# Conditioning blocks among the first projections, ScalarE evicting the RWKV preparation, and C merged inside the inverse, in a two-layer mixer kernel on one core

## The chip, the cores and the metric

The kernel runs on one NeuronCore of a Trainium2 chip. The metric is the device time of one execution in microseconds (us). TensorE (PE) multiplies matrices, VectorE (DVE) and ScalarE (ACT) do the elementwise work and empty PSUM, GpSimd (POOL) does some masks and starts small DMAs, and SyncE (SP) starts the DMAs of the weights.

## The reference

All arrays are float32, for one sequence of T = 256 tokens of width 1024. The first block projects x into four branches and their gates, merges the branches, normalizes, and adds a mixture of 32 experts with 4 per token. A second block (modulated norm, dilated attention, pooling) follows. What matters here:

```python
z = x @ w_in                                # zA | zB | zC | zD | zG
yA = rwkv7_mix(zA)                          # 8 heads of 64, token shift first
#   a = sigmoid(a0 + xa @ a2)
#   decay = exp(-exp(-softplus(-(w0 + tanh(xw) @ w2)) - 0.5))
#   kk = k * k_k;  kk = kk / max(sqrt(sum(kk * kk)), 1e-12)
#   k = k * (1 + (a - 1) * k_a)
#   state = state * w + (state @ -kk) (kk * a)^T + v k^T ;  y = state @ r
yB, yC, yD = hgrn2_mix(zB), mlstm_mix(zC), rglru_mix(zD)
merged = sum(sigmoid(zG_n) * (y_n @ w_branch_n) for n in ABCD)
x1 = layernorm(ALPHA * x + merged @ w_out)
x2 = layernorm(ALPHA * x1 + moe(x1) + ple(x1, p))
# second block, conditioned on one vector c of 1024:
shift, scale, gate = split(c @ w_ada + b_ada, 3)        # w_ada is 1024 x 3072
h = rmsnorm(x2) * norm_g * (1 + scale) + shift
out = rmsnorm(x2 + gate * (merged2(h) @ w_out2))
```

The three vectors of the conditioning (shift, scale, gate) depend on c alone and are first read in the second block (gate8 and gateB turn the gate into rows earlier).

## The kernel before

One arena of SBUF holds everything by hand-placed offsets. Each engine has one instruction stream, written out in program order, and semaphores tie them. Three ring slots hold the weight units, of 2 MB mostly. SyncE loads them in the order of the list `UNITS` (L111), and unit n waits until unit n - 3 has been used (L503 to L510). TensorE writes into two sets of four PSUM banks, each used round robin in the order of a list: `PROJ` (L121), emptied by ScalarE through `out` (L1347), and `SMALL` (L131), emptied by VectorE through `full`. A bank of either list can be written when the entry four places earlier has been copied out.

TensorE's program is: x turned; the projections of D, C and B by `ones_channels` (L627) and `ones_tokens` (L637), with the small matmuls of the branches between them; the gates of D and the merge of D (`merge`, L648); eight levels of branch B (L764), each beside one half projection of A; the B output (L778), the gate projection G C 0; the RWKV preparation; the inverse; the chunk states and outputs of A with the quarters of the gate G A; the merge of A (ending about 563 us); the output projection `mixed` (L1039), x1 and the router (L1049, L1058), the ple projections (`embed`, L1102), and the expert loop (L1158 to L1208), then the second block.

The RWKV preparation (L782 to L875 of TensorE's program) is this. Low rank products w, a and g (L793) go to `small` banks and VectorE adds the bias (L1829 to L1831). ScalarE takes the sigmoids (L1450, L1451). The squares of the key are summed over each head (L799); ScalarE takes a square root of it (L1453), and VectorE clamps and takes a reciprocal (L1857, L1858). VectorE scans the log decays (L1862, L1863), ScalarE takes three exponentials (L1455 to L1457), and VectorE multiplies them in (L1868 to L1871), signalling `A_tilde` once per product. TensorE turns three of the products to tokens (`to_tokens`, L806), which VectorE copies out (L1876), and forms NT (`pair`, L853), which VectorE masks (L1882). GpSimd multiplies NT with a level mask (L573, once per level, `NTm_ready`), TensorE turns it (X0, `turned_bank`, L875). The inverse has four levels (L883 in the loop over `l`), each of 16 X products, 16 D products and 16 transposes DT; after the first and after the second group stands one quarter of a gate projection (`gate_quarter`, L885), eight quarters of G B in all.

The conditioning has six blocks, one for each 512 columns of w_ada. `ada_rows(i)` (L820) is eight matmuls of 32 equal columns of c against 512 columns of the weight unit; its result is copied to SBUF, and `ada(i)` (L828) turns it to partitions by four matmuls with a one-column operand; VectorE adds the bias (L1818). Blocks 0 to 3 stand between the steps of the RWKV preparation, where VectorE copies the rows (L1814). Blocks 4 and 5 stand between the router's logits and the ple projections, followed by the transpose gate8 (L1082). The merge of C (`merge("C")`) stands whole, as 32 matmuls, between X0 and the inverse. c and its companions are loaded by GpSimd after the merge of D (L561 to L564).

## Time and profile before

| what | us |
| --- | --- |
| median of 3 runs | 1945.26 (1944.66 to 1947.16) |
| the profiled execution, its own time | 1947.88 |
| its span, first to last instruction | 1945.7 |
| granted TensorE clock, mean of the span | 0.975 |
| start of the RWKV preparation's part (last level of B done) | 284.42 |
| end of the inverse's fourth level | 448.47 |
| merge of A done | 563 |
| first expert matmul | 659.02 |
| last expert step done, second block starts | about 1600 |

The page gives for each engine the busy time. The timeline lists instructions in time order, with the idle time before each and the engine that ended it. The stretch table gives busy time and granted clock between two moments: clock 1.00 is 2.4 GHz and 0.50 is 1.2 GHz. A timeline row's count is in records; a matmul of 128 columns by 256 has two records.

### The profile page before, as it was taken

To read this page: it belongs to the slowest core of one execution; us is meant where nothing else is said; L and a number is where in the kernel's file an instruction comes from. 1 tells how busy PE (TensorE), PEld (TensorE's weight loads), DVE (VectorE), ACT (ScalarE), POOL (GpSimd) and SP (SyncE) were. 2 spreads that over 40 slices of the span, in tenths; PEclk is the share of its full clock that TensorE was granted. 3 is DMA by queue.
4 is the path that set the end of the run, shared out by engine and by line. 5 is a ranking of instruction groups with operands and counts; after the bars stand their busy time and mean duration, and the time that the engine had idled before them with its cause. 6 is when DMAs were issued, how large, how long until landed. Compare 5 with 4: busy or idle time off the path is not lost. (4 is left out here: it accounts for less than half of the span.)

```text
span 1945.7 us, 21418 instructions
## 1 busy us (share of the span) xinstructions
PE 1835.1 (94%) x8829; PEld 1074.9 (55%) x8829; DVE 553.8 (28%) x1037; ACT 237.2 (12%) x379; POOL 43.9 (2%) x39
## 2 busy tenths in 40 slices
PE   8999998899999999999999999999999979999998
PEld 7688886699865344333333333333333327768984
DVE  3543486555234211111111111111111130014412
ACT  0322122000100001100101101101101111011100
POOL 1000000130000000000000000000000000000000
PEclk9999998899898999999999999999999989999999
DMA  7443342512138899999999999999999975532331
GB/s 258 147 156 124 105 140 87 189 72 90 47 122 299 351 422 428 428 428 428 429 428 428 428 428 428 429 428 429 427 429 427 429 287 195 165 130 87 103 135 60
DMA packets 94139, 537.69 MB, mean 276 GB/s; under 512 B 5763, under 2 KB 15277, under 8 KB 69385
## 3 DMA queue, kind: packets, MB, share of 16 engines
q1 hardware_dynamic: 88960, 527.53, 67.4%
q10 hardware_dynamic: 3464, 4.85, 0.9%
q0 software_dynamic: 1664, 4.58, 0.8%
q8 instruction: 38, 0.62, 0.1%
q14 instruction: 13, 0.10, 0.0%
HBM read 531.18 MB, written 5.77 MB: 276 GB/s over the span
## 5 line engine op out<-in xcount | busy, mean ns | idle before, releaser
L1176 PE MATMUL small<-arena 128*64 128x512 f32 x2048 | 459.7, 597 | 44.2 <-DMA arena<-in_expert_w_gu 44.2
L1176 PEld LDWEIGHTS small<-arena 128*64 128x64 f32 x2048 | 160.0, 137 | 338.3 <-issue 248.7
L1208 PE MATMUL small<-arena 128*64 128x512 f32 x1024 | 226.8, 594 | 4.6
L2119 DVE TENSOR_SCALAR arena<-small 128x512 f32<-128x512 f32 x32 | 22.1, 692 | 721.7 <-PE small L1183 721.7
L627 PE MATMUL proj<-arena 128*128 128x256 f32 x960 | 211.5, 381 | 0.0
L627 PEld LDWEIGHTS proj<-arena 128*128 128x128 f32 x960 | 182.6, 191 | 25.7 <-issue 1.0
L1229 PE MATMUL proj<-arena 128*128 128x256 f32 x768 | 167.5, 379 | 0.0
L1229 PEld LDWEIGHTS proj<-arena 128*128 128x128 f32 x768 | 145.4, 190 | 20.3 <-issue 1.0
L1208 PEld LDWEIGHTS small<-arena 128*64 128x64 f32 x1024 | 84.7, 137 | 124.6 <-issue 124.6
L1347 ACT ACTIVATE arena<-proj 128x512 f32<-128x512 f32 (+1 forms) x76 | 45.3, 597 | 542.5 <-PE proj L885 168.3
L1485 ACT ACTIVATE arena<-arena 128x512 f32<-128x512 f32 x32 | 20.2, 630 | 548.1 <-DVE arena L2119 548.1
L1158 PE MATMUL proj<-arena 64*128 64x512 f32 x264 | 65.6, 615 | 0.7 <-ACTq L1495 0.7
L1123 PE MATMUL small<-arena 128*64 128x512 f32 x264 | 63.9, 605 | 0.0
L1238 PE MATMUL proj<-arena 128*128 128x512 f32 x128 | 59.9, 626 | 3.9 <-DVE arena L2145 3.9
L885 PE MATMUL proj<-arena 128*128 128x256 f32 x256 | 63.0, 402 | 0.0
L885 PEld LDWEIGHTS proj<-arena 128*128 128x128 f32 x256 | 50.6, 203 | 7.5
L2176 DVE TENSOR_TENSOR arena<-proj,arena 128x512 f32<-128x512 f32 (+2 forms) x24 | 13.4, 558 | 124.2 <-PE proj L1272 123.7
L648 PE MATMUL small<-arena 128*128 128x256 f32 x192 | 45.5, 401 | 3.4 <-DVE arena L1964 3.4
L1158 PEld LDWEIGHTS proj<-arena 64*128 64x128 f32 x264 | 22.7, 186 | 43.1 <-issue 41.5
L1493 ACT ACTIVATE arena<-small 128x512 f32<-128x512 f32 x32 | 19.1, 597 | 212.3 <-PE small L1208 212.3
L1238 PEld LDWEIGHTS proj<-arena 128*128 128x128 f32 x128 | 25.6, 203 | 34.7 <-issue 30.1
L648 PEld LDWEIGHTS small<-arena 128*128 128x128 f32 x192 | 38.6, 202 | 9.5 <-DVE arena L1964 3.6
(445 smaller groups left out, 1634.2 us busy)
## 6 DMA issues: line engine op xcount, KB each, us to landing
arena<-in_expert_w_gu SPq DMA_DIRECT2D x128, 2048.0 KB, 24.7
arena<-in_expert_w_down SPq DMA_DIRECT2D x64, 2048.0 KB, 20.4
arena<-in_w_in_first SPq DMA_DIRECT2D x20, 2048.0 KB, 7.8
arena<-in_w_in SPq DMA_DIRECT2D x16, 2048.0 KB, 9.1
arena<-in_w_ada SPq DMA_DIRECT2D x6, 2048.0 KB, 7.9
arena<-in_w_branch SPq DMA_DIRECT2D x4, 2048.0 KB, 7.8
arena<-in_w_out SPq DMA_DIRECT2D x4, 2048.0 KB, 8.1
bias_rows<-arena ACTq DMA_DIRECT2D x1, 4608.0 KB
```

Of the source, the lines that this page charges most:

```text
L627: mm = pe.matmul(ps[:, m * T:m * T + T], w[:, k, (2 * b + m) * P:(2 * b + m + 1) * P], XT[:, k, :], start=k == 0, stop=k == KD - 1)
L648: mm = pe.matmul(ps[:, m * T:m * T + T], w[:, k, (2 * i + m) * P:(2 * i + m + 1) * P], YT[b][:, k, :], start=k == 0, stop=k == KW - 1)
L885: mm = pe.matmul(ps[:, m * T:m * T + T], w[:, k, quarter * P:quarter * P + P], XT[:, k, :], start=k == 0, stop=k == KD - 1)
L1123: mm = pe.matmul(bank[CAP * half:CAP * half + CAP, :], PICK[:, j, :], x1[:, j, half * W:half * W + W], start=j == 0, stop=j == 1, skip_gro ...
L1158: mm = pe.matmul(acc_bank[2 * j + half][:, :], PTW[lo:lo + CAP, j * P:j * P + P], YSB[lo:lo + CAP, :], start=False, stop=False, skip_group ...
L1176: mm = pe.matmul(bank[CAP * half:CAP * half + CAP, :], XG[:, k % 4, k // 4, :], w[:, k % 2, n * D + half * W:n * D + half * W + W], start= ...
L1208: mm = pe.matmul(y_bank[CAP * half:CAP * half + CAP, :], HM[:, m, u, :], w[:, m, half * W:half * W + W], start=u == 0 and m == 0, stop=u = ...
L1229: mm = pe.matmul(ps[:, m * T:m * T + T], w[:, k, (2 * b + m) * P:(2 * b + m + 1) * P], HT[:, k, :], start=k == 0, stop=k == KD - 1)
L1238: mm = pe.matmul(ps[:, :], HT[:, k, j * P:j * P + P], w[:, k, :], start=k == 0, stop=k == KD - 1)
L1347: act.activation(dst, v, func).then_inc(sig("proj_out"), 1)
L1485: act.activation(SGH, GH, ACT.Sigmoid, scale=1.702).then_inc(sig("sig_ready"), 1)
L2119: TS(GH, gate_bank[:, :], 7.0, None, ALU.min).then_inc(sig("g_ready"), 1)
```

## The change

- The six conditioning blocks and their weight units stand among the first projections (after C q, C k, C v, C o, B f and B q). Their rows go to `proj` banks, and ScalarE copies them out. GpSimd loads c at the program's start. gate8 is turned between the first x1 transposes and the last `mixed`.
- In the RWKV preparation the low rank products, V and the three turned products go to `proj` banks and ScalarE empties them, the bias and the sigmoid of w and a in the same activations. The key norm is max(sum, 1e-24), then exp(-0.5 log), in place of square root, clamp and reciprocal. ScalarE applies the B norm (eight activations of 128x128). NT is made before At, Bt and Kt.
- G C 0 and G C 1 are cut in quarters that stand between the steps of the preparation. The merge of C is cut in four quarters that stand in levels 1 and 2 of the inverse, and every level now has three fillers.

The diff, cut to its core:

```diff
-UNITS = (["D xr", "D gate", "C q", "C k", "C if", "C v", "C o", "B f", "B q", "B i", "B g",
+UNITS = (["D xr", "D gate", "C q", "ada 0", "C k", "ada 1", "C if", "C v", "ada 2", "C o", "ada 3", "B f", "ada 4", "B q", "ada 5",
...
@@ TensorE, RWKV preparation
+            gate_quarter("G C 0", 0)
+            gate_quarter("G C 0", 1)
             pe.wait_ge(sig("proj_out"), proj_no("B i 1") + 1)
...
-            ones_channels("G C 0")
...
-                    ps = small(f"A {nm} {i}")
+                    ps = proj(f"A {nm} {i}")
...
             to_tokens("V", vA)
-            ones_channels("G C 1")
+            gate_quarter("G C 0", 2)
+            gate_quarter("G C 0", 3)
+            gate_quarter("G C 1", 0)
+            gate_quarter("G C 1", 1)
+            pe.wait_ge(sig("A_tilde"), 2)
+            pairs("NT", bA, kkA)
...
-            ada(3)
-            merge("C")
+            pe.wait_ge(sig("A_tilde"), 3)
+            for name, src in (("At", kkA), ("Bt", bA), ("Kt", kA)):
+                to_tokens(name, src)
...
@@ TensorE, router
             logits(0)
-            ada_rows(4)
             x1_turned(1)
             logits(1)
...
-            ada_rows(5)
-            ada(4)
-            ada(5)
-            pe.wait_ge(sig("small_out"), small_no("ada 5") + 1)
-            pe.transpose(small("gate8")[0:8, 0:P], MODT[:, 16:24], ident).then_inc(sig("small_full"), 1)
@@ ScalarE
+            low_rank("w", e2A, "rwkv_w0")
+            low_rank("a", aA, "rwkv_a0")
...
             rsqrt(stB[:, 1, :], "B_var", "B_rstd")
-            gates("C", 1, (0, 1))
-            act.wait_ge(sig("A_lowrank"), 1)
-            do(act.activation(e2A, e2A, ACT.Sigmoid))
-            do(act.activation(aA, aA, ACT.Sigmoid), "A_sig")
-            act.wait_ge(sig("A_kksum"), 1)
-            do(act.activation(e1A, e1A, ACT.Sqrt), "A_norm")
+            rsqrt(norm, "A_kksum", "A_norm")
             act.wait_ge(sig("A_cum"), 1)
-            do(act.activation(e1A, cumA, ACT.Exp, scale=-E_HALF))
             do(act.activation(e3A, e2A, ACT.Exp, scale=-E_HALF))
             do(act.activation(e2A, cumA, ACT.Exp, scale=E_HALF), "A_exps")
-            gates("C", 1, (2, 3))
+            do(act.activation(e1A, cumA, ACT.Exp, scale=-E_HALF), "A_exps")
+            act.wait_ge(sig("B_squared"), 1)
+            for h in range(8):
+                op = act.activation(o2B[:, h, :], o2B[:, h, :], ACT.Copy, scale=stB[:, 1, h:h + 1])
@@ VectorE
-            do(TS(e1A, e1A, 1e-12, None, ALU.max))
-            do(dve.reciprocal(e1A, e1A))
...
+            for i in range(4):
+                ada(i)
             for i in range(2):
                 n = small_no(f"C row {i}")
```

TensorE's stream among the first projections, from the D gates (L681, now L704) on to C v (L637, now L640) and the next projection. `proj` and `small` are the two sets of banks. Before:

```order
L681 MATMUL small<-arena 128x256 x8
L627 MATMUL proj<-arena 128x256 x32
L688 MATMUL proj<-arena 4x256 x16
L637 MATMUL proj<-arena 128x512 x16
L627 MATMUL proj<-arena 128x256 x64
```

Now, with L662 the conditioning rows and L670 their turning:

```order
L704 MATMUL small<-arena 128x256 x8
L662 MATMUL proj<-arena 32x512 x8
L630 MATMUL proj<-arena 128x256 x32
L670 MATMUL small<-arena 128x1 x4
L662 MATMUL proj<-arena 32x512 x8
L715 MATMUL proj<-arena 4x256 x16
L640 MATMUL proj<-arena 128x512 x16
L670 MATMUL small<-arena 128x1 x4
L662 MATMUL proj<-arena 32x512 x8
```

Each block's eight matmuls of rows now stand behind a projection, and its four one-column matmuls one projection later.

TensorE's stream in the RWKV preparation, before, from the gate projection G C 0 to the merge of C (L793 low rank, L799 key sums, L743 the turned B, L806 turned products, L836 bonus, L853 NT, L875 X0):

```order
L627 MATMUL proj<-arena 128x256 x32
L784 MATMUL small<-arena 128x40
L793 MATMUL small<-arena 128x256 x12
L799 MATMUL small<-arena 128x512 x2
L743 MATMUL small<-arena 128x128 x8
L806 MATMUL small<-arena 128x128 x8
L627 MATMUL proj<-arena 128x256 x32
L820 MATMUL small<-arena 32x512 x8
L836 MATMUL small<-arena 128x512 x2
L828 MATMUL small<-arena 128x1 x4
L820 MATMUL small<-arena 32x512 x8
L806 MATMUL small<-arena 128x128 x24
```

and, going on to the merge:

```order
L828 MATMUL small<-arena 128x1 x4
L820 MATMUL small<-arena 32x512 x8
L853 MATMUL small<-arena 128x128 x16
L828 MATMUL small<-arena 128x1 x4
L820 MATMUL small<-arena 32x512 x8
L875 MATMUL small<-arena 128x128 x16
L828 MATMUL small<-arena 128x1 x4
L648 MATMUL small<-arena 128x256 x32
```

Now, from the low rank products to the first level (L864 low rank, L870 key sums, L842 turned products, L834 gate quarters, L817 NT, L882 bonus, L779 the turned B, L899 X0, L892 inverse, L909 merge of C):

```order
L864 MATMUL proj<-arena 128x256 x12
L870 MATMUL small<-arena 128x512 x2
L842 MATMUL proj<-arena 128x128 x8
L834 MATMUL proj<-arena 128x256 x32
L817 MATMUL small<-arena 128x128 x16
L882 MATMUL small<-arena 128x512 x2
L779 MATMUL small<-arena 128x128 x8
L834 MATMUL proj<-arena 128x256 x16
L899 MATMUL small<-arena 128x128 x16
L842 MATMUL proj<-arena 128x128 x24
L892 MATMUL small<-arena 128x128 x16
L909 MATMUL small<-arena 128x256 x8
```

The conditioning is gone from this place, NT has moved ahead of the turned products, and two gate quarters stand behind the turned B. Two more stand ahead of the B output, out of these rows.

ScalarE's stream in the same place, before (L1450, L1451 sigmoids, L1453 square root, L1455 to L1457 exponentials, L1347 evictions):

```order
L1347 ACT_TABLE_LOAD
L1347 ACTIVATE arena<-proj 128x512 x2
L1450 ACTIVATE arena<-arena 128x1024
L1451 ACTIVATE arena<-arena 128x1024
L1453 ACT_TABLE_LOAD
L1453 ACTIVATE arena<-arena 128x1024
L1455 ACT_TABLE_LOAD
L1455 ACTIVATE arena<-arena 128x1024
L1456 ACTIVATE arena<-arena 128x1024
L1457 ACTIVATE arena<-arena 128x1024
L1347 ACT_TABLE_LOAD
L1347 ACTIVATE arena<-proj 128x512 x8
```

Now (L1491 low rank, L1444 and L1445 log and exp, L1505 to L1507 exponentials, L1510 the B norm):

```order
L1375 ACTIVATE arena<-proj 128x512
L1491 ACTIVATE arena<-proj,arena 128x256 x8
L1375 ACTIVATE arena<-proj 128x512 x4
L1392 ACT_TABLE_LOAD
L1444 ACTIVATE arena<-arena 128x8
L1445 ACTIVATE arena<-arena 128x8
L1444 ACTIVATE arena<-arena 128x1024
L1445 ACTIVATE arena<-arena 128x1024
L1505 ACTIVATE arena<-arena 128x1024
L1506 ACTIVATE arena<-arena 128x1024
L1507 ACTIVATE arena<-arena 128x1024
L1510 ACTIVATE arena<-arena 128x128 x8
```

The square root and its table load are gone, and eight activations and four evictions have come ahead of the exponentials.

## Rows read from the trace of the kernel before

**Rows 1.** Stretch table: length, busy PE, PEld, DVE, ACT, POOL, granted clock, DMA, GB/s
```profile
284.42:448.47 164.05, 148.24 (x882) 124.77 (x882) 96.76 (x125) 19.97 (x24) 28.73 (x9) 0.92 0.33 117
```

**Rows 2.** TensorE's timeline, 310 to 370 us: start, length, line, idle before and releaser
```profile
310.42 3.78 PE L799 MATMUL small<-arena 128*128 128x512 f32 x4 [3.48 <-DVE arena L1835]
...
314.00 1.91 PE L743 MATMUL small<-arena 128*128 128x128 f32 x8
...
316.79 13.98 PE L627 MATMUL proj<-arena 128*128 128x256 f32 x64
...
338.59 1.87 PE L828 MATMUL small<-arena 128*128 128x1 f32 x8 [4.05 <-DVE arena L1814]
...
347.87 3.65 PE L806 MATMUL small<-arena 128*128 128x128 f32 x16 [2.97 <-DVE arena L1818]
...
365.58 1.97 PE L875 MATMUL small<-arena 128*128 128x128 f32 x16 [3.15 <-POOL arena L573]
...
368.80 1.02 PE L828 MATMUL small<-arena 128*128 128x1 f32 x8 [1.24 <-DVE arena L1891]
```

**Rows 3.** Stretch table, the half-clock stretches of that part (columns as rows 1)
```profile
309.50:312.90 3.40, 2.48 (x3) 1.17 (x4) 2.39 (x3) 0.00 (x0) 0.00 (x0) 0.50 0.00 0
336.80:343.60 6.80, 5.01 (x24) 2.37 (x24) 4.16 (x5) 5.62 (x5) 0.00 (x0) 0.51 0.45 146
347.10:357.30 10.20, 9.43 (x44) 6.47 (x45) 6.17 (x11) 0.00 (x0) 0.00 (x0) 0.51 0.33 113
371.00:374.40 3.40, 3.40 (x10) 2.71 (x9) 0.02 (x1) 0.00 (x0) 3.40 (x1) 0.54 1.00 332
```

**Rows 4.** TensorE's timeline, the bias matmuls that close an expert step, two early, two later
```profile
784.35 1.09 PE L1183 MATMUL small<-arena 32*64 32x512 f32 x8
...
811.56 1.09 PE L1183 MATMUL small<-arena 32*64 32x512 f32 x8
...
898.90 1.09 PE L1183 MATMUL small<-arena 32*64 32x512 f32 x8
...
928.27 1.09 PE L1183 MATMUL small<-arena 32*64 32x512 f32 x8
```

**Rows 5.** SyncE's waits, 596 to 665 us, and the stretch table just before refilling
```profile
SPq L518 <- PE small L1102: 14.7, 1, 14.7
...
664.50:666.00 1.50, 1.50 (x10) 0.46 (x8) 0.00 (x0) 0.00 (x0) 0.00 (x0) 1.00 0.08 33
```

**Rows 6.** TensorE's timeline, after the one-column matmuls that end at 172.5
```profile
172.56 29.56 PE L627 MATMUL proj<-arena 128*128 128x256 f32 x128
```

**Rows 7.** TensorE's timeline around the router's logits, 594 to 621 us
```profile
594.13 1.92 PE L820 MATMUL small<-arena 128*32 128x512 f32 x16
...
596.90 1.09 PE L1049 MATMUL small<-arena 128*128 128x128 f32 x8 [0.85 <-DVE arena L1997]
...
603.70 3.17 PE L820 MATMUL small<-arena 128*32 128x512 f32 x16
...
611.79 9.41 PE L1102 MATMUL small<-arena 128*128 128x512 f32 x16
```

**Rows 8.** Timelines of VectorE, ScalarE and GpSimd in the RWKV preparation
```profile
312.60 0.69 DVE L1839 COPY arena<-small 128x512 f32<-128x512 f32 x1 [0.97 <-PE small L799]
...
324.57 6.56 DVE L1858 RECIPROCAL arena<-arena 128x1024 f32<-128x1024 f32 x1
...
333.68 2.87 DVE L1862 TENSOR_TENSOR_SCAN arena<-arena 128x256 f32<-128x256 f32 x4
...
342.52 1.23 DVE L1868 SCALAR_TENSOR_TENSOR arena<-arena 128x1024 f32<-128x1024 f32 x1 [2.54 <-ACT arena L1457]
...
337.89 1.28 ACT L1455 ACT_TABLE_LOAD   x1 [20.40 <-DVE arena L1863]
...
340.27 1.06 ACT L1456 ACTIVATE arena<-arena 128x1024 f32<-128x1024 f32 x1
...
360.99 4.54 POOL L573 TENSOR_TENSOR arena<-arena 128x2048 f32<-128x2048 f32 x1 [141.51 <-DVE arena L1882]
```

More of the change, by code:

```diff
@@ L707, in _ @@
             ones_channels("B q")
+            ada(4)
+            ada_rows(5)
             pe.wait_ge(sig("C_qk"), 1)
@@ L861, in copied, with gate_quarter @@
                 pe.wait_ge(sig("small_out"), small_no(f"A {name} {i}") + 1)
+            def gate_quarter(what, quarter):
+                w = unit(what)
+                b, m = divmod(quarter, 2)
+                name = f"{what[:-1]}{int(what[-1]) * 2 + b}"
+                ps = proj(name) if m == 0 else proj_bank[proj_no(name) % 4]
+                for k in range(KD):
+                    mm = pe.matmul(ps[:, m * T:m * T + T], w[:, k, quarter * P:quarter * P + P], XT[:, k, :], start=k == 0, stop=k == KD - 1)
+                if m == 1:
+                    mm.then_inc(sig("proj_full"), 1)
@@ L863, in product @@
+            pe.wait_ge(sig("A_rk"), 1)
+            for i in range(2):
+                ps = small(f"A bonus {i}")
+                pe.matmul(ps[:, :], c("headsum"), bonusA[:, 2 * i:2 * i + 2, :], start=True, stop=True).then_inc(sig("small_full"), 1)
+            turned("B yT", tB2.rearrange("p a b -> p (a b)").rearrange("p (j n) -> p j n", j=TT), "B_normed")
+            gate_quarter("G C 1", 2)
+            gate_quarter("G C 1", 3)
             def product(name, lhs, rhs, i):
@@ L1373, in _, with ada_rows @@
             channels("C q", cz[:, 0:4, 3:])
+            def ada_rows(i):
+                out(f"ada rows {i}", ADAROW[:, i % 2, :])
             act.wait_ge(sig("D_gates"), 1)
@@ L1843, in _ @@
+            for m in range(KW):
+                do(dve.tensor_tensor_scan(cumA[:, m, :], c("reset64"), e2A[:, m, :], 0.0, ALU.mult, ALU.add))
+            do(TTn(e2A, cumA, e2A, ALU.subtract), "A_cum")
+            dve.wait_ge(sig("proj_out"), proj_no("A a 1") + 1)
             do(STT(bonusA, aA, -1.0, over(pv("rwkv_k_a"), T), ALU.add, ALU.mult))
             do(STT(kA, bonusA, 1.0, kA, ALU.add, ALU.mult))
+            dve.wait_ge(sig("A_norm"), 1)
+            do(TTn(kkA, kkA, norm, ALU.mult))
@@ L1845, in _, with masked @@
+            do(TTn(bA, kkA, aA, ALU.mult))
+            dve.wait_ge(sig("A_exps"), 1)
+            do(STT(kkA, kkA, -1.0, e3A, ALU.mult, ALU.mult), "A_tilde")
+            dve.wait_ge(sig("A_exps"), 2)
+            do(TTn(bA, bA, e2A, ALU.mult), "A_tilde")
             do(TTn(bonusA, rA, kA, ALU.mult))
             do(TTn(bonusA, bonusA, over(pv("rwkv_r_k"), T), ALU.mult), "A_rk")
+            def masked(name, dst, mask, banks=range(4)):
+                for i in banks:
+                    do(TTn(dst[:, 4 * i:4 * i + 4, :], tiles(full(f"A {name} {i}"), P), along(c(mask), 4), ALU.mult), "small_out")
@@ L1847, in _ @@
+            masked("NT", NT, "strict64")
+            do(TTn(kA, kA, e2A, ALU.mult), "A_tilde")
+            do(TTn(rA, rA, e1A, ALU.mult), "A_tilde")
+            for i in range(2):
+                do(TTn(bonusA[:, 2 * i:2 * i + 2, :], tiles(full(f"A bonus {i}")), vA[:, 2 * i:2 * i + 2, :], ALU.mult), "small_out")
             for i in range(2):
@@ L2018, in _ @@
             x1_turned(0)
+            do(dve.tensor_copy(G8, full("gate8")[0:8, 0:P]), "small_out")
             residual(1, 1)
```

321 lines of the change are left out of this document (158 added, 163 removed), and 7 rows, old and new, of the table PROJ.

## The prediction

> **What bounds the kernel now.** I read the timeline of TensorE first, then the stretch table, then the SyncE waits. Up to the expert loop at 659.02 us TensorE is almost always busy, so every idle gap and every stretch at half clock there is time. The largest loss is the RWKV preparation with the inverse, 284.42 to 448.47 us: 164.05 us long, TensorE busy for 148.24, so idle for 15.8 [rows 1]. The idle time stands ahead of the key sums (3.48), the turned rows of conditioning (4.05 and 1.24), Bt (2.97) and X0 (3.15) [rows 2], each ended by VectorE or GpSimd. After each gap TensorE is granted 1.2 GHz for a while: four stretches of 3.4, 6.8, 10.2 and 3.4 us with 2.48 + 5.01 + 9.43 + 3.40 = 20.3 us busy [rows 3], and half of that, 10.2 us, is lost.
>
> The expert loop is bound otherwise. Its first steps come 811.56 - 784.35 = 27.2 us apart, which is TensorE's own work, later ones 928.27 - 898.90 = 29.4 us, which is the time of 12 MB of weights [rows 4]. Does an earlier TensorE help a loop bound by DMA? I think so. The loads of expert 0 wait for TensorE to release ring slots (14.7 us at one of them), and just before the first release in the loop the DMA engines are at 0.08 [rows 5]. The stream therefore has no backlog and starts when TensorE starts. What is saved ahead of 659 us comes off the end, one for one.
>
> **Part 1: the preparation.** I take away from 164.05 the idle 15.8, the clock's 10.2, and four conditioning blocks. One block is 1.92 us of rows [rows 7] and 1.02 of turning [rows 2], 2.9 together, so 11.6 for four. That leaves 126.4 us of dense work. The gates G C and the merge of C stay within the stretch, only in other places, and cost the same.
>
> How much idle comes back? The first half gate moves ahead of the B output. From 284.42 to the end of the row at 316.79's start there are 32.4 us before; less the idle 0.9 and 3.48, the 1.2 lost to the clock and the turned B (1.91) they hold 24.9, of which G C 0 is 13.98 [rows 2]; B output, low rank, key sums and V are the other 10.9. In the new order six quarters of 3.5 us stand with them, so NT is reached at 284.4 + 10.9 + 21.0 = 316.3 (times of the old trace; the early blocks shift all of it). VectorE's chain runs beside this. The key sums end at 301.2. Eviction with the clamp 0.7, scans 2.9, a difference and two products 3.7, then four products of 1.23 [rows 8] with their gaps, 5.0: the second `A_tilde` comes at 313.5. The reciprocal's 6.56 us [rows 8] is what is gone from it. ScalarE beside it: four evictions, a table load 1.28 and two activations of 1.06 [rows 8] give the norm at about 306.7, before VectorE wants it (308.5), and the first two exponentials at 309, also in time. So NT waits for nothing, with 2.8 us to spare.
>
> No row has ScalarE's 128x256 activations out of PSUM with a bias pointer. The nearest are the 1.06 of 1024 columns, and VectorE's 0.69 for 512 columns out of PSUM [rows 8]. I bound one at 0.3 and 0.7 and take 0.42. Eight of them then add between -1.0 and 2.2 us to a chain with 2.8 to spare, so the sum holds at either end. The eight 128x128 activations of the B norm are bounded by 0.2 and 0.6, so 1.6 to 4.8 us from 310; TensorE wants the result at about 321, cover at either end. The DMAs of c move to the head of GpSimd's queue, where they delay the LRU weights by under 2 us, and those are needed at 55.
>
> One gap stays. X0 is followed by 24 transposes only, 3.0 us by X0's 1.97 for 16 [rows 2]. GpSimd's mask for level 1 starts some 0.8 us after X0 and takes 4.54 [rows 8], so TensorE waits about 2.3 us. Before, the merge of C hid this. The third filler in each level costs nothing extra and hides nothing, as the four levels have no idle now. The part is then 126.4 + 2.3 = 128.7 us long: **35.3 us less**.
>
> **Part 2: conditioning among the projections.** Six blocks of 2.9 us come in ahead of 284.42: **17.4 us more**. Their rows are copied by ScalarE, whose queue there has gaps; each copy is asked for one projection (14 us) later. VectorE's turned blocks 0 to 3 are placed ahead of the C rows and block 4 ahead of the masks of C, so VectorE stands there for TensorE up to about 151 us while the silu products are already done; the next thing TensorE wants from it is C's weights some 30 us later. SyncE's list gets six units of 2 MB, each asked for when the unit three places back is used, 15 us or more ahead of use. I cost these waits at zero.
>
> **Part 3: the router.** From 603.70 to 611.79 stand block 5, both turnings, gate8 and two waits [rows 7]: 8.1 us leave. Block 4's rows (1.92, at 594.13) free nothing, as the transposes after them wait for x1 anyway (0.85 [rows 7]); that wait grows to 2.8. VectorE loses a copy of 0.7 ahead of the XT copies, 0.3 of gain. The first ple projection took 9.41 us for eight matmuls of 512 columns, against 13.98 / 2 = 7.0 at full clock [rows 2, 7]: 2.4 lost, of which I give back 0.9, since the half clock after the x1 wait stays and now falls on that projection. gate8 puts 0.2 on the path. **9 us less.**
>
> **The sum.** -35.3 + 17.4 - 9 = -26.9. The remaining wait of 2.3 us is about as long as gaps after which the clock fell, so I add 1: **-26 us**. The profiled execution took 1947.88 us, 2.6 above the median, so it would take 1921.9, and the median becomes 1945.3 - 26 = **1919.3**.
>
> **Rivals.** (a) *The expert stream does not move with the router.* Then part 3 is worth nothing: 1928. Against it stands the DMA share of 0.08 before the first release. Chance 0.09.
>
> (b) *The early blocks run or leave the clock low.* After the one-column matmuls of C's denominator, the next 128 records took 29.56 us against 2 x 13.98 [rows 2, 6], 1.6 lost. Each block has four such matmuls, a third as many. If each costs as much, six cost 9.6: 1929. The Trainium skill, "TensorE: Matmul & The Clock Gate", Part 1 on the HAM clock gate, says that the default state is throttled and activity releases it, which makes this rival likelier; the trace agrees only for the longer run of one-column matmuls. Chance 0.13.
>
> (c) *The margin of 2.8 us is not there*, because ScalarE, which now carries 12 evictions in order with the norm and the exponentials, is late. NT then waits, and the clock falls after it: with 6 us of wait, and a 10.2 us stretch at half clock as in rows 3, 11 us come back: 1930. Chance 0.08.
>
> (d) *Slower: the blocks hold the clock down.* The 10.2 us stretch [rows 3] had a block in it. If each of the six now drew such a stretch over its neighbours, 5.1 us would be lost each time, 30.6 in all: 1950. It decides from 26 / 6 = 4.3 us per block. Against it: around each block stand 14 us projections without gaps, and the block itself has none. Chance 0.05.
>
> (e) *No net change:* the chain stays as late as before in other places, so that only the blocks have moved: 1945. Chance 0.05.
>
> **How the numbers follow.** The forecast has 0.60. Its own range is 1914 (no loss to the clock, 2.3 us gap hidden) to 1925. With (a), (b) and (c) the range 1913.5 to 1931 holds 0.90 of the cases by my list; the tails of each leave it at 8 in 10. A measurement of this kernel tells 0.2%, 3.9 us, from no change: faster 0.90, same 0.05, slower 0.05.
>
> **What would show it.** Right: the start of the B output about 24 us later than before (17 and the two quarters); no wait of NT; one wait of about 2 us at the first level; the fourth level's end 18 us earlier, the loop's start 27 us earlier; steps of 29.4 us as before. Wrong: granted clock under 0.97 before 280 us, a wait ahead of NT, or a loop that ends later than its start says.

## The result and the profile after

| | kernel before | kernel after |
|---|---|---|
| median of 4 runs | 1946.05 us | 1929.43 us |
| lowest to highest | 1944.66 to 1947.16 | 1929.17 to 1931.28 |
| profiled execution | 1947.88 | 1929.45 |
| its span | 1945.7 | 1927.7 |
| mean granted clock | 0.975 | 0.979 |

The ratio is 0.9923, 95% interval 0.9912 to 0.9935. The change is faster and the time lies inside the predicted range, but by the interval it gave 12.6 to 17.1 us where 26 were forecast. All comparisons below are of spans and starts in the profiled executions, unless they say "median".

Line numbers have moved: the mask of GpSimd is L576 now (L573 before), the row projections of conditioning L662 (L820), their turning L670 (L828), the products NT L817, the first inverse level L892, the ple projection L1130 (L1102), the bias matmuls at the end of an expert step L1211 (L1183).

The stretch table of the kernel after, columns as rows 1. The first row is the stretch that answers to [rows 1], the preparation with the inverse, from the end of B's cross product to the end of level 4. The second goes on to the first expert step; before, it went from 448.47 to 659.02 and was 210.55 us long. The other three are stretches at half clock.

```profile
302.10:438.00 135.90, 128.24 (x787) 115.59 (x786) 80.88 (x99) 25.37 (x45) 29.63 (x9) 0.97 0.22 79
438.00:640.77 202.77, 195.17 (x1024) 137.78 (x1022) 82.86 (x153) 15.10 (x24) 5.55 (x10) 0.92 0.46 157
240.50:243.90 3.40, 3.40 (x12) 2.81 (x12) 2.71 (x4) 0.00 (x0) 0.00 (x0) 0.57 0.00 0
356.50:363.30 6.80, 5.95 (x29) 5.95 (x30) 1.74 (x3) 0.00 (x0) 0.80 (x1) 0.53 0.01 2
639.80:646.60 6.80, 6.80 (x18) 1.80 (x18) 1.19 (x5) 0.00 (x0) 1.08 (x2) 0.53 0.94 364
```

Read the lengths and the starts. The stretch begins at 302.10 instead of 284.42: **+17.7**. It lasts 135.90 instead of 164.05: **-28.15**. The router part lasts 202.77 instead of 210.55: **-7.8**. The sum is -18.25, which is where the loop starts (640.77 against 659.02), and the span is 18.0 shorter. The granted clock of the preparation rose from 0.92 to 0.97, and its idle time fell from 15.8 to 135.90 - 128.24 = 7.7 us. Nearly all of that is one wait.

TensorE's timeline of the kernel after, from NT to the first level (start, length, line, tiles, shape, idle before and what ended it):

```profile
333.01 2.82 PE L817 MATMUL small<-arena 64*128 64x128 f32 x32
...
347.44 0.66 PE L899 MATMUL small<-arena 128*128 128x128 f32 x4 [0.38 <-DVE arena L1917]
347.93 2.78 PE L842 MATMUL proj<-arena 128*128 128x128 f32 x24
357.35 5.06 PE L892 MATMUL small<-arena 128*128 128x128 f32 x22 [6.63 <-POOL arena L576]
```

NT has no wait in brackets: it was reached without one. TensorE is then done with the token transposes at 350.71 and waits **6.63 us** for GpSimd's mask. The half clock (granted clock 0.53 from 356.5 to 363.3) comes with it: level 1's first 32 matmuls take 6.48 us in all, against 3.73 for the next 32. Why is the mask so late? VectorE's and GpSimd's timelines of the same kernel:

```profile
334.27 2.87 DVE L1906 TENSOR_TENSOR arena<-small,arena 128x512 f32<-128x512 f32 x4 [0.73 <-PE small L817]
337.17 1.22 DVE L1909 TENSOR_TENSOR arena<-arena 128x1024 f32<-128x1024 f32 x1
338.43 5.42 DVE L1910 TENSOR_TENSOR arena<-arena 128x1024 f32<-128x1024 f32 x1
...
347.53 2.29 DVE L1922 TENSOR_TENSOR arena<-arena 128x2048 f32<-128x2048 f32 x1
349.86 2.87 DVE L1924 TENSOR_TENSOR arena<-small,arena 128x512 f32<-128x512 f32 x4
```

```profile
337.22 5.55 POOL L576 TENSOR_TENSOR arena<-arena 128x2048 f32<-128x2048 f32 x1 [327.85 <-DVE arena L1906]
352.80 4.49 POOL L576 TENSOR_TENSOR arena<-arena 128x2048 f32<-128x2048 f32 x1 [10.03 <-DVE arena L1924]
```

L1909 and L1910 are the same operation on the same shape, `kA*e2A` and `rA*e1A`. One took 1.22 us and the other 5.42. Between them GpSimd's mask runs from 337.22 to 342.77, in 5.55 us where its twin took 4.49. The numbers fit one engine at a time. The mask gets going when L1909 ends (338.39 + 4.49 = 342.88, recorded end 342.77), and L1910 when the mask ends (342.77 + 1.23 = 344.00, recorded end 343.85). From there everything is late by the same amount: DTa's addition, X0's eviction (ended 352.73), the second mask (ended 357.29), level 1.

The Trainium skill, "SBUF — State Buffer", section "Who interferes with whom", says that a VectorE instruction with two SBUF inputs contends with a GpSimd instruction that reads SBUF, and that the shared ports are an exclusive lock, so that the loser stands fully blocked. These rows agree with it, in both directions. The kernel before had the same two products (its L1870 and L1871) while GpSimd was idle; its mask for level 1 stands below them:

```profile
345.05 1.23 DVE L1870 TENSOR_TENSOR arena<-arena 128x1024 f32<-128x1024 f32 x1
346.31 1.22 DVE L1871 TENSOR_TENSOR arena<-arena 128x1024 f32<-128x1024 f32 x1
...
370.90 4.51 POOL L573 TENSOR_TENSOR arena<-arena 128x2048 f32<-128x2048 f32 x1 [5.38 <-DVE arena L1891]
```

X0 ended at 365.58 + 1.97 = 367.55 there [rows 2], so this mask came 3.3 us behind it, while C's merge kept TensorE busy.

In the expert loop, the bias matmuls that close a step, two early and two later, after:

```profile
657.35 1.09 PE L1211 MATMUL small<-arena 32*64 32x512 f32 x8
...
684.55 1.09 PE L1211 MATMUL small<-arena 32*64 32x512 f32 x8
...
1174.50 1.09 PE L1211 MATMUL small<-arena 32*64 32x512 f32 x8
...
1203.86 1.09 PE L1211 MATMUL small<-arena 32*64 32x512 f32 x8
```

The steps are 27.2 us apart at first and 29.36 later, as in [rows 4]; the whole loop has moved by 18 us and nothing else. The later pace is that of the weights: each of those steps has a wait of TensorE for them, as in the rows of e6_ple_early below.

### The profile page after: what moved, and what is told of

Its sections match the earlier page's. It is cut to its first block and busy times, and to the rows that moved or that the text cites. A ratio compares the mean times of both kernels' runs of the same rounds, so it can differ in the third digit from the quotient of the medians.

```text
span 1927.7 us, 21410 instructions
## 1 busy us (share of the span) xinstructions
PE 1826.7 (95%) x8829; PEld 1072.8 (56%) x8829; DVE 536.0 (28%) x1014; ACT 246.8 (13%) x407; POOL 44.8 (2%) x39
## 5 line engine op out<-in xcount | busy, mean ns | idle before, releaser
L1375 ACT ACTIVATE arena<-proj 128x512 f32<-128x512 f32 (+1 forms) x92 | 54.3, 599 | 554.9 <-PE proj L834 166.5
L834 PE MATMUL proj<-arena 128*128 128x256 f32 x384 | 90.0, 391 | 0.0
L834 PEld LDWEIGHTS proj<-arena 128*128 128x128 f32 x384 | 73.9, 197 | 10.3
L892 PE MATMUL small<-arena 128*128 128x128 f32 x320 | 40.1, 287 | 6.6 <-POOL arena L576 6.6
L892 PEld LDWEIGHTS small<-arena 128*128 128x128 f32 x320 | 39.9, 203 | 7.3 <-POOL arena L576 6.9
```

Source lines behind the costliest of these rows:

```text
L834: mm = pe.matmul(ps[:, m * T:m * T + T], w[:, k, quarter * P:quarter * P + P], XT[:, k, :], start=k == 0, stop=k == KD - 1)
L892: mm = pe.matmul(ps[:, m * P:m * P + P], lhs[:, n, :], rhs[:, n, :], start=True, stop=True)
L1375: act.activation(dst, v, func).then_inc(sig("proj_out"), 1)
```

## The experiments

Theory: two engines block each other in SBUF, which puts the level 1 mask late; where TensorE waits, half clock follows; all that TensorE is earlier at the loop comes off the end. The rivals differ from run to run and stand with each. All runs are edits of the kernel after (1929.43). The kernel before was run with each group of four: medians 1945.63, 1944.93 and 1945.23.

| run | median us | lowest to highest | ratio to before, 95% interval |
|---|---|---|---|
| e1_order | 1925.76 | 1917.87 to 1926.27 | 0.9892 (0.9873 to 0.9910) |
| e2_c_whole | 1914.77 | 1913.88 to 1916.81 | 0.9843 (0.9830 to 0.9857) |
| e3_sqrt | 1934.48 | 1933.98 to 1936.33 | 0.9948 (0.9934 to 0.9962) |
| e4_no_blocks | 1912.79 | 1910.83 to 1913.29 | 0.9830 (0.9817 to 0.9844) |
| e5_b_first | 1919.15 | 1918.05 to 1920.06 | 0.9871 (0.9854 to 0.9888) |
| e6_ple_early | 1924.88 | 1921.13 to 1929.88 | 0.9894 (0.9877 to 0.9910) |
| e7_order_ahead | 1915.85 | 1913.71 to 1917.21 | 0.9851 (0.9833 to 0.9868) |
| e8_all | 1907.41 | 1904.61 to 1909.58 | 0.9811 (0.9795 to 0.9826) |
| f0_same | 1932.69 | 1928.55 to 1934.29 | 0.9936 (0.9922 to 0.9949) |
| f1_pad14 | 1928.51 | 1927.41 to 1932.71 | 0.9924 (0.9911 to 0.9937) |
| f2_pad27 | 1931.20 | 1922.33 to 1933.56 | 0.9922 (0.9905 to 0.9938) |
| f3_dve8 | 1925.79 | 1924.22 to 1926.92 | 0.9901 (0.9887 to 0.9915) |

**e1_order: the two products kept clear of GpSimd**

```diff
+            do(TTn(kA, kA, e2A, ALU.mult), "A_tilde")
             masked("NT", NT, "strict64")
-            do(TTn(kA, kA, e2A, ALU.mult), "A_tilde")
-            do(TTn(rA, rA, e1A, ALU.mult), "A_tilde")
...
             do(TTn(DTa, NTm, along(ident, 16), ALU.add))
+            do(TTn(rA, rA, e1A, ALU.mult), "A_tilde")
```

> The changed kernel (1929.4 us) with VectorE's kA*e2A moved ahead of the masking of NT and rA*e1A moved behind DTa's addition, so that GpSimd reads nothing while either product runs. Theory (VectorE and GpSimd block each other: the product at L1910 took 5.42 us beside GpSimd's level mask instead of 1.23, and the mask 5.55 instead of 4.5): both products take 1.23, the mask 4.5, X0 is evicted 2 to 3.5 us earlier, the 6.63 us wait of TensorE at level 1 falls to about 3.2, and the half clock after it is smaller or gone: 1923 to 1926 us. Rival (the wait is the price of moving the merge of C: a mask of 4.5 us after X0 that nothing covers, whatever VectorE does): wait stays at 6 to 7, time 1929 +- 1. Rival (the 5.42 us are the tile's placement or a wait inside the instruction, not GpSimd): the product takes about 5.4 us at its new place too.

Its VectorE timeline (L1908 and L1922 are the two products), then GpSimd's, then TensorE's:

```profile
332.30 1.23 DVE L1908 TENSOR_TENSOR arena<-arena 128x1024 f32<-128x1024 f32 x1
...
336.46 1.42 DVE L1911 TENSOR_TENSOR arena<-small,arena 128x512 f32<-128x512 f32 x2
...
341.07 2.29 DVE L1921 TENSOR_TENSOR arena<-arena 128x2048 f32<-128x2048 f32 x1 [1.11 <-POOL arena L576]
343.40 1.23 DVE L1922 TENSOR_TENSOR arena<-arena 128x1024 f32<-128x1024 f32 x1
344.78 2.87 DVE L1924 TENSOR_TENSOR arena<-small,arena 128x512 f32<-128x512 f32 x4 [0.16 <-PE small L899]
```

```profile
336.51 4.53 POOL L576 TENSOR_TENSOR arena<-arena 128x2048 f32<-128x2048 f32 x1 [327.11 <-DVE arena L1906]
347.73 4.50 POOL L576 TENSOR_TENSOR arena<-arena 128x2048 f32<-128x2048 f32 x1 [6.69 <-DVE arena L1924]
```

```profile
345.82 2.78 PE L842 MATMUL proj<-arena 128*128 128x128 f32 x24
352.29 6.39 PE L892 MATMUL small<-arena 128*128 128x128 f32 x32 [3.68 <-POOL arena L576]
```

Both products take 1.23 us and the first mask 4.53. The wait fell from 6.63 to 3.68, so the collision was worth 2.95 us of it. Another 0.8 us went ahead of the wait: from NT's start to the token transposes TensorE takes 14.10 us here and 14.92 in the kernel after, where X0 waits for VectorE. The half clock did not go: 32 matmuls of level 1 took 6.39 us, where e2_c_whole has them in 3.73. The median is 3.7 us lower than the kernel after. In this profile 1.3 us of the earlier start of level 1 are not the edit's, since NT itself starts at 331.72 instead of 333.01. The mutual blocking is shown; both rivals fall.

**e2_c_whole: C's merge ahead of the inverse again**

```diff
+            merge("C")
             for l in range(1, 5):
                 pe.wait_ge(sig("NTm_ready"), l + 1)
...
-                if l == 1:
-                    merge_quarter("C", 0)
-                elif l == 2:
...
+                gate_quarter(f"G B {(l - 1) // 2}", 2 * ((l - 1) % 2))
```

VectorE's side and the order of the PSUM banks follow; the third filler of each level goes.

> The changed kernel with one part undone: the merge of C whole (14 us of TensorE) ahead of level 1, and two fillers in each level again. Theory (that part of the change was a loss, since the merge had covered X0's eviction and the mask): the 6.63 us wait at level 1 goes, and with it the half clock after it (about 2.9 us), the levels themselves have no idle with two fillers: 1919 to 1921 us. Rival (the levels need the third filler): the wait goes, but levels 1 to 4 get idle of 1 us or more each, and the time is 1925 or more. Rival (the part does nothing on the whole): 1929.

TensorE's, VectorE's and GpSimd's timelines of this run:

```profile
349.20 2.78 PE L841 MATMUL proj<-arena 128*128 128x128 f32 x24
351.96 14.05 PE L650 MATMUL small<-arena 128*128 128x256 f32 x64
365.85 3.73 PE L891 MATMUL small<-arena 128*128 128x128 f32 x32
```

```profile
356.47 2.67 DVE L1638 TENSOR_TENSOR arena<-arena 128x512 f32<-128x512 f32 x1
```

```profile
354.07 4.52 POOL L575 TENSOR_TENSOR arena<-arena 128x2048 f32<-128x2048 f32 x1 [10.04 <-DVE arena L1902]
```

No wait stands in brackets at level 1 or in the levels behind it (the kernel after has one more, 0.64 us in level 2), and level 1 runs at full clock. The last group of the same pair products (L817 of the kernel after) starts at 463.34 against 472.05, though NT came 1.3 us later (334.27 against 333.01): 10.0 us less between the two, which is the 9.5 expected and the 0.64. The median fell by 14.7. What goes beyond the theory lies at the head of the loop in the profile: the granted clock is 1.00 from 627 to 647 us here, where the kernel after has a stretch of half clock (639.80 in the table above). Moving C's merge into the levels was a loss, then, of some 10 us by the trace. The DVE row is a second case of blocking: 2.67 us instead of 0.69, up to the mask's end at 358.59 and its own work behind it.

**e3_sqrt: the key norm by Sqrt and reciprocal again**

```diff
-                do(TS(norm[:, 2 * i:2 * i + 2, :], tiles(full(f"A kk {i}")), 1e-24, None, ALU.max), "small_out")
+                do(dve.tensor_copy(norm[:, 2 * i:2 * i + 2, :], tiles(full(f"A kk {i}"))), "small_out")
...
-            rsqrt(norm, "A_kksum", "A_norm")
+            act.wait_ge(sig("A_kksum"), 1)
+            do(act.activation(norm, norm, ACT.Sqrt), "A_norm")
...
+            do(TS(norm, norm, 1e-12, None, ALU.max))
+            do(dve.reciprocal(norm, norm))
```

> The changed kernel with one part undone: the key norm by Sqrt on ScalarE with a clamp and a reciprocal (6.56 us before) on VectorE. Theory (NT is reached without a wait, with 2 to 3 us to spare, and the reciprocal is on its chain): 7.3 us more on VectorE ahead of the first A_tilde, NT waits 4 to 5.5 us, half clock for some us after it; the wait at level 1 is then no longer (its chain moves with it): 1934 to 1938 us. Rival (another chain, ScalarE's evictions and exponentials, is as late as VectorE's, so the reciprocal is hidden): under 1931.

TensorE's timeline of this run, NT and level 1:

```profile
339.74 5.13 PE L817 MATMUL small<-arena 64*128 64x128 f32 x32 [5.32 <-DVE arena L1903]
...
365.89 6.08 PE L892 MATMUL small<-arena 128*128 128x128 f32 x32 [6.02 <-POOL arena L576]
```

As the theory said: NT now waits 5.32 us and runs at half clock (5.13 us instead of 2.82), and the level 1 wait shrinks by only 0.6 to pay for it. From the start of the four gate quarters ahead of NT (L834, 320.44 here and 319.10 in the kernel after) to level 1 it takes 7.2 us more (45.45 against 38.25). So the log and exp were a gain, by the trace. The median says less: it is 5.05 us above the kernel after, but only 1.8 above f0_same, which is the kernel after once more, and this profile lacks the half clock at the head of the loop.

**e4_no_blocks: conditioning left out**

```diff
-         + [f"ada {i}" for i in range(4)] + ["C row 0", "C row 1", "C col", "ada 4"] + [f"C S {h}" for h in range(4)]
+         + ["C row 0", "C row 1", "C col"] + [f"C S {h}" for h in range(4)]
...
-            for i in range(4):
-                ada(i)
+            do(dve.tensor_copy(MODT, PV2[:, 16:40]))
```

> The changed kernel without its six conditioning blocks: the second block's modulation is then the bias alone, and the 12 MB of those weights are not loaded. Theory (a block costs its own 2.7 us of TensorE and nothing besides, but the delay of them all let the 3.8 us wait at L800 be followed by a half clock stretch that the kernel before did not have): 16 us less from the blocks, up to 1.8 us more if the stretch of half clock ahead of the B branch goes: 1911.5 to 1913.5 us. Rival (each block holds the clock or the queues back as well): 20 us or more less, under 1909. Rival (later waits take part of it back, as the expert stream is not ready so early): over 1915, with a wait on a DMA in the first expert steps.

The median fell by 16.64, or 2.77 us per block, in the band of the theory. In the profile the matmuls just ahead of the expert loop (L1178 of the kernel after) start 16.57 us earlier (619.92 against 636.49). That is what a block's own work costs, 1.92 + 0.95 with the two overlapping a little, and no more. One part of the theory fell: half clock still follows the wait ahead of B (granted clock 0.57 from 223 to 227), so the blocks' delay was not what brought it in.

**e5_b_first: B's level 0 products ahead of the diagonal evictions**

```diff
+            level_products(0)
             for j in range(TT):
                 do(TTn(aB[:, 4 * j:4 * j + 4, :], tiles(full(f"B diag {j}"), P), along(ident, 4), ALU.mult), "small_out")
```

> The changed kernel (1929.4 us) with one VectorE order changed ahead of the B branch: the two products of B's level 0 before the eviction of B's two diagonal banks. Theory (TensorE's 3.82 us wait at L800 is VectorE's order, and the half clock behind it, 8.37 instead of 7.07 us for the next projection, is that wait's): wait under 1 us, half clock behind it gone, 3.0 to 4.8 us less: 1924.6 to 1926.4 us. Rival (the half clock stands there for another reason, as the same wait had none behind it in the kernel before): wait gone, stretch stays, 1926 to 1927. Rival (the wait turns up again at level 1 of B): 1929.

The wait ahead of B, in the kernel after and then in this run:

```profile
238.58 2.48 PE L800 MATMUL small<-arena 128*128 128x128 f32 x16 [3.82 <-DVEq L1868]
240.85 8.37 PE L630 MATMUL proj<-arena 128*128 128x256 f32 x32
```

```profile
233.54 2.05 PE L800 MATMUL small<-arena 128*128 128x128 f32 x16 [0.68 <-DVEq L1858]
235.43 7.07 PE L630 MATMUL proj<-arena 128*128 128x256 f32 x32
```

The wait is 3.1 us shorter and the half clock behind it gone. So in this kernel the half clock there goes with the wait, and the two rivals fall; but the same wait of 3.82 us stood in the kernel before (ahead of its L764, at 222.41) with a granted clock of 1.00 behind it, so a wait of that length does not always bring half clock. From the end of the work ahead of the wait to B's second group of level products this profile takes 4.8 us less (9.48 against 14.29), the upper end of the theory. But the median fell by 10.3, over twice that. Of the rest the profile has 1.9 us ahead of every place that the edit touches, where the kernel's first projection (L688) took 7.17 us instead of 9.17, and 3.6 us again at the head of the loop, which has no half clock in this run: the first step's bias matmuls (L1211) come 67.3 us after the second half of x1 is turned (L1083), against 70.9 in the kernel after. Whether the shorter wait brought the latter about or chance did, this run doesn't tell.

**e6_ple_early: ple's first matmuls in the router's wait**

```diff
             logits(0)
+            w = unit("ple 0")
+            ps = small("ple 0")
+            for k in range(KD):
+                mm = pe.matmul(ps[:, :], XT[:, k, 0:P], w[:, k, :], start=k == 0, stop=k == KD - 1)
+            mm.then_inc(sig("small_full"), 1)
             x1_turned(1)
```

> The changed kernel with ple's first eight matmuls (128x512, 3.55 us) moved from behind the router logits to between the first and the second half of them, where TensorE waits 2.70 us for the second token tile of x1. Theory (the wait costs its own length and the half clock behind it, 13.7 us of it in the changed kernel): the 2.70 us wait goes, 2.7 us less, and up to 5 us more as the half clock shrinks: 1922 to 1926.7 us. Rival (the time is set by the stream of expert weights, not by TensorE, at this place): 1929. Rival (half clock there does not come from the wait): 1926.7, the stretch as long as before.

The first row below is the start of the expert loop's matmuls and the second a step's last part, in the kernel after; then the same two of this run:

```profile
640.77 16.64 PE L1204 MATMUL small<-arena 128*64 128x512 f32 x64
...
818.53 3.65 PE L1204 MATMUL small<-arena 128*64 128x512 f32 x16 [1.25 <-DMA arena<-in_expert_w_gu]
```

```profile
641.43 13.95 PE L1211 MATMUL small<-arena 128*64 128x512 f32 x64
...
818.50 3.65 PE L1211 MATMUL small<-arena 128*64 128x512 f32 x16 [1.24 <-DMA arena<-in_expert_w_gu]
```

The 2.70 us wait went, but the one behind it grew from 0.90 to 1.48, so 2.1 us of waiting are saved; half clock still stands from 598 to 610 us (granted clock 0.57). The median fell by 4.5, with executions 8.8 us apart. More than those 2.1 us isn't shown, nor the theory's second part (half clock that shrinks with the wait). The profiled execution is the slowest of the five, with a span 0.4 us longer than that of the kernel after. TensorE reached the first x1 transposes 4.0 us later (576.90 against 572.92), ahead of the edit. It made that good, and the step's bias matmuls came 2.04 us earlier (655.31 against 657.35), only because the head of the loop had no half clock: 13.95 us instead of 16.64. And this lead was lost again: at 818.5 us both kernels wait for weights and go on at the same time. What is saved at the head of the loop does not always come off the end.

**e7_order_ahead: e1_order and one quarter of C's merge ahead of level 1**

```diff
+            merge_quarter("C", 0)
             for l in range(1, 5):
                 pe.wait_ge(sig("NTm_ready"), l + 1)
```

> The reordered products of e1_order (1925.8 us) and one quarter of C's merge (3.5 us of TensorE) ahead of level 1 instead of in it. Theory (what is left of the wait, 3.68 us, is the mask of level 1, and any 3.5 us of work beside it is enough): wait under 0.3 us, half clock behind it gone, so 5 to 7 us less than e1_order: 1918.5 to 1921 us; the difference to e2_c_whole (1914.8 us) is then only chance of the clock. Rival (e2_c_whole was faster for another reason, the two fillers instead of three in each level): 1922 or more even with no wait.

TensorE's timeline:

```profile
350.84 3.62 PE L909 MATMUL small<-arena 128*128 128x256 f32 x16
354.70 7.41 PE L892 MATMUL small<-arena 128*128 128x128 f32 x64 [0.24 <-POOL arena L576]
```

The wait is 0.24, level 1 at full clock (64 matmuls in 7.41), and the median, 1915.85, is that of e2_c_whole within their spread. So beside the reordered products 3.5 us of work ahead of level 1 is enough, and three fillers instead of two in levels 2 to 4 make no difference that can be seen.

**e8_all: the version meant to beat both**

e2_c_whole, e1_order, e5_b_first and e6_ple_early together.

> All together: e1_order's products, e2_c_whole's merge of C ahead of level 1, e5_b_first and e6_ple_early, the version meant to be faster than both kernels. Theory (each removed wait of TensorE ahead of the expert loop comes off the end one for one, with the half clock behind it): from e2_c_whole's 1914.8 us 3.0 to 4.8 and 2.7 to 7.7 us less: 1902 to 1909 us. Rival (the stream of expert weights becomes the bound when TensorE is earlier): the loop starts as early as that but its steps are 29.4 us from the first on, and the end is at 1911 or later.

The median is 1907.41, in the band: 22.0 us under the kernel after and 37.5 under the one before. The loop's steps are 27.2 and then 29.4 us as ever, five of the first kind as in the kernel after, so even 22 us earlier the stream of weights is not what holds its start. The four edits were not taken out of it one by one; their single medians fell by 3.7, 14.7, 10.3 and 4.5, which is 33 in all, more than the 22 that came; two of them shorten the same wait.

**f0_same, f1_pad14, f2_pad27: the kernel itself, and with useless work at 152 us**

```diff
                 ps = small(f"C S {h}")
+                for _ in range(h < 2):
+                    pe.matmul(ps[:, 0:T], qk[:, 4 + h, 0:P], qk[:, h, :], start=True, stop=True)
+                    pe.matmul(ps[:, T:T + P], qk[:, 4 + h, P:T], qk[:, h, P:T], start=True, stop=True)
```

(f2_pad27: `range(1)`.)

> The changed kernel itself once more, to see how far its own executions lie apart. e1_order gave 1917.87 us once and 1924 to 1926 us four times, and e5_b_first came out 10 us faster where 3.1 us of wait had gone. Theory (stretches of half clock that follow no wait fall differently from one execution to the next): median 1927 to 1931 us, with single executions up to 8 us apart. Rival (they are fixed by the program): all five within 2 us.

> The changed kernel with two of the four pairs of matmuls of C's scores done twice at 152 us (1.4 us more work of TensorE, the same result). Theory (where the half clock falls depends on when TensorE reaches a place, not only on the waits): the difference to the changed kernel is not 1.4 us but off it by 3 us or more, either way, and the list of half clock stretches differs. Rival (the stretches belong to places in the program): 1.4 us more, 1929 to 1932 us, with the same stretches shifted by 1.4 us.

> As f1_pad14 with all four pairs done twice (2.7 us more work). Theory: off 1929.4 + 2.7 by 3 us or more in one of the two kernels f1_pad14 and f2_pad27 at least, and not growing evenly. Rival: 1931 to 1933 us.

The same program gave 1928.55 to 1934.29 here, 5.7 us apart, with a median 3.3 above that of the first four runs. Added work of 1.4 us gave 1928.51 and 2.7 us gave 1931.20: 4.2 and 1.5 below f0_same. No run shows the added work as its own size, since it is smaller than the chance. That half clock falls differently from execution to execution is shown by f0_same: its profile is at half clock from 494 to 505 us (granted clock 0.53), and that of the kernel after, the same program, only from 496 to 503 (0.51). That it hangs on when TensorE reaches a place is not shown: f1_pad14 is 2.3 us off 1929.4 + 1.4 and f2_pad27 0.9 us off 1929.4 + 2.7, both under the 3 us that the theory asked for. But one stretch is missing in f1_pad14, that behind the one-column matmuls of C's denominator. The projection behind them, in the kernel after, then in f1_pad14:

```profile
188.72 29.56 PE L630 MATMUL proj<-arena 128*128 128x256 f32 x128
```

```profile
188.49 27.87 PE L630 MATMUL proj<-arena 128*128 128x256 f32 x128
```

e4_no_blocks has 27.87 there too, and a stretch of half clock at 124 to 128 us that no other profile has. So the 1.7 us are not the price of those matmuls wherever they stand.

**f3_dve8: 5.5 us more for VectorE ahead of the key sums**

```diff
             for j in range(TT):
+                ps = tiles(full(f"B o {j}"), P)
+                for _ in range(4):
+                    do(dve.tensor_copy(o2B[:, 4 * j:4 * j + 4, :], ps))
```

> The changed kernel with VectorE copying B's output banks five times instead of once: eight copies of 0.69 us, 5.5 us, which is what the eight evictions of the RWKV rows (w, a, g, V) that ScalarE took over would cost VectorE. The result is the same. Theory (VectorE has 2.3 us idle ahead of the key sums and NT 2.0 us to spare, so most of the 5.5 us are absorbed): NT waits under 1.5 us and the time is 1929 to 1932 us, that is, ScalarE's evictions were worth 0 to 2 us. Rival (VectorE is the bound of this chain throughout): NT waits 3.5 us and half clock follows: 1934 or more.

TensorE's timeline of this run:

```profile
334.52 2.82 PE L817 MATMUL small<-arena 64*128 64x128 f32 x32 [0.38 <-DVE arena L1903]
...
360.10 5.40 PE L892 MATMUL small<-arena 128*128 128x128 f32 x32 [6.63 <-POOL arena L576]
```

NT waits 0.38 us: the 5.5 us are absorbed, as the theory had it. The median is 3.6 us *under* the kernel after, which neither had. Level 1 starts 2.75 us later than in the kernel after (1.1 of them stood there at 301 us already, ahead of the edit), yet the first L1211 is 1.4 us earlier (655.91 against 657.35). The half clock at the head of the loop is missing in this run. In this order, then, ScalarE's eight evictions bought no time that can be seen. This is a stand-in for the evictions, not their undoing, which wasn't tried.

## Why the prediction was right and wrong

**Bounds and the loop: right.** The loop's start moved by 18.25 us and the span by 18.0, and e8_all shows the same for 22 us more. Rival (a), a stream that doesn't move, is refuted, and so is (e), no net change. One for one has a limit all the same: the 2 us lead of e6_ple_early at the first step was gone by the seventh.

**Part 2, +17.4: right.** The B branch's end came 17.7 us later, of it 16.6 for six blocks by e4_no_blocks. The rest is the new half clock ahead of B (8.37 instead of 7.07 us). Rival (b) put a loss of 1.6 behind each block; the only half clock between the blocks and 300 us that was not there before stands behind a wait of VectorE's making, and the row from which (b) took its 1.6 is itself not constant (29.56 us, but 27.87 in f1_pad14 and e4_no_blocks). Rival (d), blocks that hold the clock down at 4.3 us or more each, is refuted by 2.77.

**Part 1, -35.3: this is the step that failed.** It gave -28.15, 7.2 us less. Its first half held: NT did not wait, and the margin was 2.0 us where 2.8 were worked out (second `A_tilde` done at 331.03, NT at 333.01), so rival (c) did not come. ScalarE's 128x256 evictions took 3.16 us for eight, 0.40 each, against 0.42 taken.

The term that failed is "TensorE waits about 2.3 us" at level 1. It waited 6.63. Of the missing 4.3, 2.95 are the blocking of VectorE and GpSimd (e1_order). The other 1.4 are an order I did not follow: the text had the mask start 0.8 us after X0, but X0's eviction stands behind DTa's addition (and in e1_order behind `rA*e1A` too), so the mask starts 1.9 us after the token transposes begin even there (345.82 and 347.73), and these cover 2.8 us of it, not 3.0. The trace of the kernel before had that order to read: its mask came 3.3 us behind X0. With two waits that had no term, 0.38 in X0 and 0.64 in level 2, the idle time is 7.7 us instead of 2.3, 5.4 more. Another 2.9 us are half clock behind the wait (6.48 us for level 1's first 32 matmuls, 3.73 in e2_c_whole); the sum had charged 1 us for it.

That makes 8.3, and 7.2 are missing, because another term was wrong the other way. [rows 3] ends its first stretch of half clock at 312.90, but the clock stayed low, and TensorE busy, for 3.4 us more:

```profile
312.90:316.30 3.40, 3.40 (x14) 2.53 (x13) 2.23 (x3) 1.16 (x1) 0.00 (x0) 0.53 0.00 0
```

So 1.6 us more than the 10.2 were lost to the clock before, and the 126.4 us called dense work held them. The kernel after has 128.24 - 2.9 = 125.3. A part of it stood in the 10.9 us of other work ahead of NT, which is why TensorE came there 1 us sooner than worked out and the margin was 2.0. These two errors partly cancelled, by luck.

The error of method is plain. The VectorE work between NT and the mask of level 1 (two products, the bonus, B's gating, DTa's addition) had no term. The only price at hand for such a product, 1.23 us, came from rows in which GpSimd was idle, and the 4.54 for the mask from a row beside which VectorE ran no product of two SBUF tiles. And I wrote that C's merge "hides nothing" in its new place without asking what it had hidden in its old one beyond 2.3 us.

**Part 3, -9: nearly right**, -7.8. The wait for x1 came out at 2.70 (2.8 expected). The first ple projection still took 9.44 us, so the 0.9 given back did not come.

**The sum.** -26.9 and 1 for the clock were forecast, -18.0 came. The sign was right and the median lies in the range, at its upper end. That is luck in part: the forecast's own range ended at 1925, and the upper part was there for rivals (a), (b) and (c), none of which came. Of the signs listed, the start of the B output (23.7 us later), NT without a wait, the steps of 29.4 us and a granted clock of 0.99 before 280 us came; the fourth level's end was 10.5 us earlier and not 18, the loop's start 18 and not 27.

## What to carry to other kernels

When work is moved, ask what it was hiding and price that chain as it will then run, with every engine's neighbours: a duration read beside an idle GpSimd is not the duration beside a busy one. Keep VectorE products of two SBUF tiles clear of GpSimd reads, or place them where nobody waits. A few microseconds of TensorE work put just ahead of a known wait are worth the wait and, in e2_c_whole and e7_order_ahead, the half clock behind it too; but judge a 3 us edit by its waits in the trace, since six executions of one program lay 5.7 us apart.

## What the runs showed of the hardware

- VectorE and GpSimd shut each other out where VectorE multiplied two SBUF tiles beside GpSimd's product of two: 5.42 instead of 1.23 us and 2.67 instead of 0.69 for VectorE, 5.55 instead of 4.5 for GpSimd. The 5.42 or 5.43 is there in all nine profiles with this order of VectorE besides that of the kernel after. VectorE's operations with one input in PSUM kept their time beside a mask: L1911 of e1_order took 1.42 us for two, 0.69 each with the gap, with the mask running from 336.51.
- The clock is a source of spread by itself. A stretch of half clock at the head of the loop (6.8 us at 639.80, 3.4 lost) with no wait ahead of it was there in the profiles of the kernel before (at 657), the kernel after, e1_order, e4_no_blocks, f0_same, f1_pad14 and f2_pad27, half as long in e8_all (at 620), and not in those of e2_c_whole, e3_sqrt, e5_b_first, e6_ple_early, e7_order_ahead and f3_dve8. What decides it stays open: of those without it, TensorE turns x1 later than in the kernel after in e3_sqrt and f3_dve8 (594.58 and 589.79 against 586.45) and earlier in e2_c_whole (579.13), so it isn't a matter of early or late. At a kernel's start there is another: the first projection (32 records at 11 us) took 7.17 us in five profiles, f0_same among them, and 9.17 to 9.50 in the other nine, that of the kernel after among them. The Trainium skill, "TensorE: Matmul & The Clock Gate", Part 1, notes that the number of slow matmuls at the start of one kernel varies from run to run; these rows agree.
- ScalarE's table load took 1.28 us in the kernel after (ACT_TABLE_LOAD at 319.96), and the next activation stood 0.02 us behind it.
